# Neighbourhood attention outputs computed by features, with probabilities divided first, in a two-layer hybrid encoder

## What is computed

```python
s = jnp.einsum('brqhd,brkwhd->bhrqkw', qg, k_band) * (d ** -0.5) + bias
s = jnp.where(in_win[:, None, :], s, -jnp.inf)
p = jax.nn.softmax(s.reshape(B, H, rows, GRID_W, kh * GRID_W), axis=-1).reshape(s.shape)
o = jnp.einsum('bhrqkw,brkwhd->brqhd', p.astype(v.dtype), v_band)
...
mixed = jnp.concatenate([ml_out, na_out, gla_out], axis=-1).astype(h.dtype)
return mixed @ w_out
```

## Time and profile before

| | us |
|---|---|
| median of 3 runs (lowest, highest) | 880.56 (879.75, 881.09) |
| profiled execution | 878.24 |
| its span, first to last instruction | 876.3 |
| TensorE busy in the span | 861.8 |
| VectorE busy | 596.0 |
| ScalarE busy | 496.1 |
| mean granted TensorE clock | 0.998 of full speed |

### The profile page before, as it was taken

The page is one execution under the profiler, slowest core; times in us unless marked ns, Lnnn a source line. Parts: engine busy times, 40 slices in busy tenths (PEclk is TensorE's granted clock), DMA queues, the critical chain, the costliest instruction groups (busy, mean ns, idle before and its releaser), DMA issues.

```text
span 876.3 us, 14948 instructions
## 1 busy us (share of the span) xinstructions
PE 861.8 (98%) x6338; PEld 798.1 (91%) x6338; DVE 596.0 (68%) x820; ACT 496.1 (57%) x689; POOL 14.3 (2%) x35
## 2 busy tenths in 40 slices
PE   8999999999999999999999999999999899999997
PEld 8999998889889999999999999988898899999996
DVE  6887678757657666666577885887665666656655
ACT  7954663658647445445567546745755645445444
POOL 5000000000000000000000000000000000000000
PEclk9999999999999999999999999999999999999999
DMA  9735452364255555555448254335435365555541
GB/s 329 201 102 177 156 178 103 112 226 144 97 193 190 195 190 195 192 191 194 145 140 257 72 171 165 127 115 192 135 109 191 127 212 190 193 196 190 192 169 48
DMA packets 114665, 146.78 MB, mean 168 GB/s; under 512 B 10600, under 2 KB 94760, under 8 KB 114600
## 3 DMA queue, kind: packets, MB, share of 16 engines
q1 hardware_dynamic: 114456, 145.57, 49.7%
q10 hardware_dynamic: 144, 0.26, 0.1%
HBM read 144.77 MB, written 1.05 MB: 166 GB/s over the span
## 4 chain that ended last, share of the span: by engine, by line
PE 92%; ACT 3%; DVE 3%; issue 1%; DMA 0%; ACTq 0%; DVEq 0%
PE bank L665 26%; PE bank L666 25%; PE bank L667 25%; PE bank L706 4%; PE bank L743 2%; PE bank L832 2%; DVE wlo L1455 2%; PE bank L1017 2%; ACT whi L1096 1%; ACT yhi L1119 1%; PE bank L872 1%; PE bank L762 1%; PE bank L849 1%; DVE ylo L1710 1%; PE bank L882 1%
## 5 line engine op out<-in xcount | busy, mean ns | idle before, releaser
L1455 DVE TENSOR_TENSOR wlo<-raw,whi 128x2048 fp32r<-128x2048 f32 (+3 forms) x144 | 306.2, 2133 | 106.1 <-ACT whi L1096 105.2
L1096 ACT ACTIVATE whi<-raw 128x2048 fp32r<-128x2048 f32 (+3 forms) x144 | 257.4, 1793 | 53.5 <-PE bank L667 48.4
L665 PE MATMUL bank<-yhi,whi 128*128 128x256 f32 x704 | 195.1, 277 | 0.5 <-DVE ylo L1471 0.5
L666 PE MATMUL bank<-ylo,whi 128*128 128x256 f32 x704 | 194.6, 276 | 0.0
L667 PE MATMUL bank<-yhi,wlo 128*128 128x256 f32 x704 | 194.6, 276 | 0.0
L665 PEld LDWEIGHTS bank<-yhi,whi 128*128 128x128 f32 x704 | 132.2, 188 | 1.6 <-issue 0.7
L666 PEld LDWEIGHTS bank<-ylo,whi 128*128 128x128 f32 x704 | 132.2, 188 | 0.8
L667 PEld LDWEIGHTS bank<-yhi,wlo 128*128 128x128 f32 x704 | 132.2, 188 | 0.0
L665 PE MATMUL bank<-xhi,whi 128*128 128x256 f32 x320 | 91.4, 286 | 2.2 <-DVE wlo L1455 1.2
L665 PE MATMUL bank<-whi,xhi 128*128 128x512 f32 (+2 forms) x256 | 90.1, 352 | 0.0
L667 PE MATMUL bank<-xhi,wlo 128*128 128x256 f32 x320 | 88.9, 278 | 0.0
(11 more groups left out here) (268 smaller groups left out, 1373.1 us busy)
## 6 DMA issues: line engine op xcount, KB each, us to landing
raw<-in_w_up SPq DMA_DIRECT2D x44, 1024.0 KB, 5.0
raw<-in_w_down SPq DMA_DIRECT2D x22, 1024.0 KB, 4.8
raw<-in_w_in SPq DMA_DIRECT2D x10, 1024.0 KB, 7.3
raw<-in_w_xk SPq DMA_DIRECT2D x8, 1024.0 KB, 5.1
raw<-in_w_xv SPq DMA_DIRECT2D x8, 1024.0 KB, 4.9
raw<-in_w_out SPq DMA_DIRECT2D x8, 1024.0 KB, 4.8
raw<-in_w_xq SPq DMA_DIRECT2D x8, 1024.0 KB, 5.7
raw<-in_w_xo SPq DMA_DIRECT2D x8, 1024.0 KB, 4.9
```

The source lines that it names most:

```text
L665: mm(o, s_hi, m_hi, start=first, stop=False, skip_group_check=True)
L666: mm(o, s_hi, m_lo, start=False, stop=False, skip_group_check=True)
L1096: A(weight(whi, gu), raw[:, gu % RING, 0:SIZE[gu]], ACT.Copy).then_inc(hi_done, 1)
L1455: tt(weight(wlo, gu), raw[:, gu % RING, 0:SIZE[gu]], weight(whi, gu), ALU.subtract).then_inc(lo_done, 1)
```

## The change

- Output products. `nao` is no longer one tile a head. Heads (0, 1), (2, 3) and (4) share tiles `nao0`, `nao1`, `nao2`, made at hh = 3, 5 and 6, ahead of that step's transposes. Stationary is `nav` of the head (128 x 64), moving are the transposed probabilities of all 256 queries; the even head's output goes to PSUM partitions 0 to 63, the odd one's to 64 to 127, so features lie on partitions.
- Divisions. VectorE divides the probabilities in SBUF (`shares_of`, two instructions of 128 x 256 a head) before the transposes, which wait for `npn_ready` in place of `np_ready`. The division of the outputs goes.
- Mixer's pair. ScalarE copies each `nao` tile, with the reversal, to `yna_hi` (in the place of `naq`), VectorE subtracts to `yna_lo` (in the place of `nak`, `heads_lo`). `tmb` is no longer transposed for k = 3 and 4, and k = 5 only feeds its upper 64 partitions. `yhi`/`ylo` are made for k = 0, 1, 2, 5, 6, 7; `wo0` begins with k = 3.
- Order. `split_hi` and `split_lo` of the next keys move up by a step (in the second layer `xk3` to hh = 0). The decay exponentials of ScalarE move from hh = 1 to hh = 2, behind the exponentials of heads 2 and 3. VectorE's denominators and head sum move from hh = 0 to hh = 2. In the second layer the GLA decay products and tails move from hh = 2 and 3 to hh = 4, the first pair ahead of the fifth head's division, the rest behind it; in the first layer they stand at hh = 2. `denominators`, `heads_sum`, `decayed` and `tails` hold the same instructions as before.

```diff
+        if h in NA_OUT:
+            p = NA_OUT.index(h)
+            job(f"nao{p}", 4 + p % 2)
         if 1 <= h <= NAH:
             job(f"nat{h - 1}", 2 + (h - 1) % 2)
-        if h >= 2:
-            job(f"nao{h - 2}", 4 + (h - 2) % 2)
...
+NA_OUT = (3, 5, 6)
+NA_PAIRS = ((0, 1), (2, 3), (4,))
+NA_K = range(3, 6)
...
+        def operand(group, k):
+
+            if group == "mx" and k in NA_K:
+                return yna_hi[:, k - 3, :], yna_lo[:, k - 3, :]
+            return tuple(x[:, k, :] for x in PAIR[group])
+
+        def mixed(k):
+
+            r = slice(64, P) if k == 5 else slice(0, P)
+            return (r,) + tuple(x[r] for x in operand("mx", k))
+
+        MIXED_K = (0, 1, 2, 5, 6, 7)
...
+                def input_is(group, kk):
+                    if group == "mx" and kk in NA_K:
+                        is_drained(pe, l, f"nao{kk - 3}")
+                    if group != "mx" or kk in MIXED_K:
+                        lo_is(pe, l, group, kk)
...
+                    if hh in NA_OUT:
+                        p = NA_OUT.index(hh)
+                        is_drained(pe, l, f"nat{NA_PAIRS[p][-1]}")
+                        free(f"nao{p}")
+                        for jt in range(TT):
+                            for g in NA_PAIRS[p]:
+                                r = slice(64 * (g % 2), 64 * (g % 2) + 64)
+                                last = mm(bank(f"nao{p}")[r, 0:T], nav[:, jt, g * DH:(g + 1) * DH], npt[:, g % 2, jt].rearrange("p a b -> p (a b)"),
+                                          start=jt == 0, stop=jt == 1, skip_group_check=True)
+                        last.then_inc(te_done, 1)
                     if 1 <= hh <= NAH:
                         g = hh - 1
-                        pe.wait_ge(np_ready, NAH * l + g + 1)
+                        pe.wait_ge(npn_ready, NAH * l + g + 1)
...
-                    if hh >= 2:
-                        g = hh - 2
-                        is_drained(pe, l, f"nat{g}")
-                        free(f"nao{g}")
-                        for t in range(TT):
-                            for jt in range(TT):
-                                last = mm(bank(f"nao{g}")[:, t * DH:(t + 1) * DH], npt[:, g % 2, t, jt, :],
-                                          nav[:, jt, g * DH:(g + 1) * DH], start=jt == 0, stop=jt == 1)
+                                last = nc.tensor.transpose(bank(f"nat{g}", TT, TT, P)[:, jt, t, :], np_[:, g % 2, t, jt * P:(jt + 1) * P], ident[:])
...
+                        if k not in MIXED_K:
+                            continue
...
-                for n in range(2):
-                    tm_unit(f"wo{n}", (f"wo{n}0", f"wo{n}1"), 512, "mx", n == 0)
+                tm_half("wo0", "a", ("wo00", "wo01"), 512, "mx", True, ks=(3,), first=3, ends=None)
+                tm_half("wo0", "a", ("wo00", "wo01"), 512, "mx", True, ks=(0, 1, 2), first=3, ends=2)
+                tm_half("wo0", "b", ("wo00", "wo01"), 512, "mx", True)
+                tm_unit("wo1", ("wo10", "wo11"), 512, "mx")
...
+                    if hh in NA_OUT:
+                        p = NA_OUT.index(hh)
+                        r = slice(0, 64 * len(NA_PAIRS[p]))
+                        is_filled(act, l, f"nao{p}")
+                        A(forwards(yna_hi[r, p, :]), backwards(bank(f"nao{p}")[r, 0:T]), ACT.Copy).then_inc(na_hi_ready, 1)
...
-                    if hh == 1:
-                        if l == 0:
-                            split_hi("xk1")
-                        else:
-                            split_hi("xk3")
-                        act.wait_ge(bc_ready, l + 1)
-                        A(b1[:], zc, ACT.Exp, scale=1.0 / 16).then_inc(eb_ready, 1)
-                        A(b3[:], zc, ACT.Exp, scale=-1.0 / 16).then_inc(eb_ready, 1)
...
+                    if hh == 2:
+                        act.wait_ge(bc_ready, l + 1)
+                        A(b1[:], zc, ACT.Exp, scale=1.0 / 16).then_inc(eb_ready, 1)
+                        A(b3[:], zc, ACT.Exp, scale=-1.0 / 16).then_inc(eb_ready, 1)
...
+                        split_hi("xk3" if l else "xk1")
                         take("gg1")
...
+                for k in MIXED_K:
                     is_filled(act, l, f"mx_{k % 4}")
-                    if k >= 4:
+                    if k - 4 in MIXED_K:
                         lo_is(act, l, "mx", k - 4)
-                    for r, v in mixed_parts(k):
-                        last = A(forwards(yhi[r, k, :]), v(turned_bank(l, "mx", k)[r, :]), ACT.Copy, scale=pcol[r, R_MG + k:R_MG + k + 1])
-                    last.then_inc(xhi_ready, 1)
+                    r, hi, _ = mixed(k)
+                    A(hi, turned_bank(l, "mx", k)[r, :], ACT.Copy, scale=pcol[r, R_MG + k:R_MG + k + 1]).then_inc(xhi_ready, 3 if k == 5 else 1)
...
+                def shares_of(g):
+                    dve.wait_ge(np_ready, NAH * l + g + 1)
+                    link(V.reciprocal(nsum[:, 2 * g:2 * g + 2], nsum[:, 2 * g:2 * g + 2]))
+                    for t in range(TT):
+                        last = ts(np_[:, g % 2, t, :], np_[:, g % 2, t, :], nsum[:, 2 * g + t:2 * g + t + 1], None, ALU.mult)
+                    last.then_inc(npn_ready, 1)
+
+                def heads_lo(p):
+                    dve.wait_ge(na_hi_ready, 3 * l + p + 1)
+                    r = slice(0, 64 * len(NA_PAIRS[p]))
+                    drain(tt(forwards(yna_lo[r, p, :]), backwards(bank(f"nao{p}")[r, 0:T]), forwards(yna_hi[r, p, :]), ALU.subtract))
...
-                    if hh == 2:
-                        dve.wait_ge(eb_ready, 2 * l + 2)
-                    if hh >= 2:
-                        g = hh - 2
-                        dve.wait_ge(np_ready, NAH * l + g + 1)
-                        link(V.reciprocal(nsum[:, 2 * g:2 * g + 2], nsum[:, 2 * g:2 * g + 2]))
-                        is_filled(dve, l, f"nao{g}")
-                        for t in range(TT):
-                            last = ts(tmb[:, t, ML + g * DH:ML + (g + 1) * DH], bank(f"nao{g}")[:, t * DH:(t + 1) * DH],
-                                      nsum[:, 2 * g + t:2 * g + t + 1], None, ALU.mult)
-                        drain(last)
...
+                        for g in NA_PAIRS[0]:
+                            shares_of(g)
                         split_lo("xk2" if l else "xk0")
                         memory_lo("mem", l, range(KT))
-                        link(tt(hr[:, :, 0:DH], hr[:, :, 0:DH], den[:].rearrange("p (n o) -> p n o", o=1).broadcast_to([P, 24, DH]), ALU.mult))
-                        link(tt(mlh, hraw[:, :, 0, :, 0:DH], hraw[:, :, 1, :, 0:DH], ALU.add))
+                        split_lo("xk3" if l else "xk1")
                     if hh == 1 and l == 0:
-                        split_lo("xk1")
+                        split_lo("xk2")
                     if hh == 2:
-                        if l:
+                        denominators()
+                        for g in NA_PAIRS[1]:
+                            shares_of(g)
+                        heads_sum()
+                        if l == 0:
+                            decayed(0)
+                            decayed(1)
+                            tails()
                             split_lo("xk3")
-                        is_drained(dve, l, "gk")
-                        for d in range(2):
-                            tt(b2[:, 2 * d:2 * d + 2, :], gq[:], b1[:, 2 * d:2 * d + 2, :], ALU.mult)
-                            ins = tt(b3[:, 2 * d:2 * d + 2, :], gk[:], b3[:, 2 * d:2 * d + 2, :], ALU.mult)
-                        link(ins)
-                        if l == 0:
-                            split_lo("xk2")
                     if hh == 3:
-                        for d in range(2):
-                            cv = lambda v: v[:, 2 * d:2 * d + 2, :].rearrange("p a (c n) -> p (a c) n", n=LG)
-                            e = cv(b1)[:, :, (LG - 1) * (1 - d):(LG - 1) * (1 - d) + 1]
-                            last = tt(cv(b4), cv(b3), e.broadcast_to([P, 2 * NCH, LG]), ALU.mult)
-                        last.then_inc(qd_ready, 1)
-                        if l == 0:
-                            split_lo("xk3")
+                        heads_lo(0)
                     if hh == 4 and l == 0:
                         head_squares(mlh, sq, 0, MLH)
                     if hh == 4:
+                        if l:
+                            decayed(0)
+                        shares_of(4)
+                        if l:
+                            decayed(1)
+                            tails()
                         split_lo("xv0a")
-                    if hh == 5 and l:
-                        head_squares(mlh, sq, 0, MLH)
+                    if hh == 5:
+                        if l:
+                            head_squares(mlh, sq, 0, MLH)
+                        heads_lo(1)
...
                 drain(V.tensor_copy(kty[:].rearrange("p a b c -> p (a b) c"), bank("kt1", 4, P)[:, :, 0:32]))
+                heads_lo(2)
...
```

(46 more changed lines are left out.)

29 lines of the change are left out of this document (16 added, 13 removed).

## The result

The changed kernel takes 882.43 us (median; 880.30 to 883.73), the kernel before 879.94 (878.07 to 882.41) beside it: a ratio of 1.0027, interval 1.0016 to 1.0037. It is slower by 0.27%, 2.4 us by the ratio and 2.5 between the medians. The prediction said 878.8, 1.7 under the kernel before, and a range of 877.2 to 881.0; 882.43 lies above it.

The account below looks back on a forecast made before the run. TensorE, busy 98% of the span, was taken to bound the kernel. First layer -0.8 - 0.76, second +0.6 - 0.74, together -1.7: 880.56 - 1.7 = 878.8 us, range 877.2 to 881.0.

Parts of the forecast that it names:

- Part 1: Output products, each layer: three groups of 1.10 replace five of 0.84; TensorE's stream 0.8 us shorter, range 0.4 to 1.3.
- rival (b): Pair groups' two halves don't run side by side: 1.95 for 1.10 us a group, 881.4 us in all; chance 0.09.
- Part 2: Divisions ahead of the transposes: nothing charged; head 4 in the first layer has only 0.7 us of cover.
- Rival (c): Head 4's division late, or ScalarE's new copies hold its exponentials; TensorE also stops in first layer: 879.6 us; chance 0.14.
- Part 3: Key low parts one head ahead: in the second layer a 0.5 us TensorE stop goes, with 0.2 of shorter waits.
- Part 4: VectorE's chain late in second layer: TensorE stops 2.1 to 2.2 us for kt1 before state products, 0.6 lost.
- Rival (d): The 2.2 us stop in the second layer drops the clock to 1.2 GHz behind it: 883 us; chance 0.05.
- Part 5: Mixer's split and projection: four transposes and a stop go, 0.76 us in the first layer, 0.74 in the second.

Follow-up runs that it names:

- e3: The changed kernel with the GLA decay products and tails back at hh = 2 in the second layer: 881.03 us, ratio 1.0023 to the kernel before.
- e7: e2 with VectorE's split of xk3 back from hh = 0 to hh = 2 in the second layer: 877.46 us, ratio 0.9986 to the kernel before.
- e1: The changed kernel with the low part of nao1 right behind the decay tails in the second layer: 879.47 us, ratio 1.0001 to the kernel before.
- e2: e1 with the second layer's head squares behind the state products and ScalarE's root behind its xv0_0 copy: 875.80 us, ratio 0.9951 to the kernel before.
- e5: e2 with a pair's four products issued head by head, not in turn: 875.91 us, ratio 0.9972 to the kernel before.
- e4: The changed kernel with 19 unused identity products in TensorE's stop before kt0, second layer: 879.84 us, ratio 0.9994 to the kernel before.

## Why the prediction was wrong

**What bounds, and the method.** Right. TensorE's stream decides: its stretches account for the whole difference of the two spans.

**Part 1, the output product.** The mechanism was right, the sum in part by luck. Timeline of TensorE in the changed kernel, L0, a pair and the single head with what follows each:

```profile
123.23 1.08 PE L890 MATMUL bank<-arena,nav 128*64 128x256 f32 x8
124.24 0.66 PE L899 MATMUL bank<-ident,arena 128*128 128x128 f32 x4
139.34 1.08 PE L890 MATMUL bank<-arena,nav 128*64 128x256 f32 x4
140.35 0.66 PE L926 MATMUL bank<-ident,arena 128*128 128x128 f32 x4
```

A group takes 1.01 to the next, forecast 1.10. That eight passes of a pair take no longer than four of the single head shows the halves side by side: rival (b) is out. L0 gained 0.75, forecast 0.8, but out of two sizes that were off and cancel: in the chain of the changed kernel the three groups are 0.09 cheaper each than forecast, and the transposes behind each take 0.58 or 0.59 where they take 0.44 behind other products (0.45 for L900 behind the old output product). That is 0.43 to 0.45 a layer; the prediction allowed 0.1. 4.20 - 3.03 - 0.43 is 0.74.

**Part 2, divisions ahead of the transposes.** Right: no transpose of the changed kernel waits for a division in either layer. The cover was as thin as forecast: in L0 the fifth head's division is done at 135.44 and its transposes begin at 135.93, 0.5 later; in L1 it is 564.18 and 564.58. e3 and e7 put more of VectorE's work ahead of divisions (3.6 us of GLA products, a split of some 2.2), and TensorE stopped 1.71 and 1.2. Rival (c) did not come, but its place was real.

**Part 3, key low parts.** No wait at the keys, as forecast. The loop of L1 came out 1.74 shorter where the parts gave 1.5 (0.8 and 0.7). In e7 the old place costs 1.2, at the transposes.

**Part 4, VectorE in L1: here the prediction failed.** The chain itself was added up well. I had the low part of `nao1` done near 570.8 (561.1 + 0.1 + its steps down to the low part, 9.6), and it was done at 571.09, in a profile whose scores start 0.40 later. The step that failed is the next one: "copies kt0 and kt1 0.8". I let VectorE take the two copies behind the low part and let TensorE run on to the state products, stopping only for `kt1`: "a stop of 2.1 to 2.2". I never asked whether TensorE may write `kt0` at all. The bank plan has the answer (`job` gives each tile its bank, `free` waits for the tile before it there): `kt0` follows `nao1` in bank 5, and `kv0` follows `nao2` in bank 4. Before, the last reader of those tiles was the short division of the outputs, long done; after, it is the low part, which the same chain has at its end. So the stop stands ahead of `kt0`, not ahead of the state products, and the 2.7 us of work between the two (568.34 to 571.04 before) no longer fill it. By my own numbers it could have been had: state products reached at 569.5, so the first transposes at 566.8; low part done at 570.8; a stop of 4.0. Measured 4.20. The forecast stop itself was real: with the bank free in time, e1 has it at 2.22, all but 0.33 of it for the copy of `kt1`.

**Rival (d), the clock.** I gave it 0.05, since a stop of 2.2 seemed short against the 3.3 us of idle time at the end of the kernel. With 4.20 that argument turns round. Its mechanism was right and its size near: "four microseconds of work would take eight", measured 3.2 more. That its 883 lies so close to 882.43 is luck, since it leaves out 2.1 us of stop and 0.8 of gain that came on top. And e1, with one stop of 2.22, shows the fall in its profile, so even my own 2.2 was not safe. The 3.3 of the earlier trace rows is when the clock fell, read as if it were the least that brings it down; the rows do not say that.

**Part 5, mixer and projection.** Right in kind, too small: -1.18 and -1.15 for -0.76 and -0.74. Two sizes were off. The stop ahead of the second half stands as 0.32 in the idle column, and I took it at that. Timeline of TensorE in the kernel before, the last product ahead of it:

```profile
172.09 0.39 PE L667 MATMUL bank<-whi,ylo 128*128 128x512 f32 x1
```

From there to 172.79 are 0.70, where 0.23 is usual from product to product, and the next one follows after 0.34: the stop cost some 0.6. The transposes, timeline of TensorE in the changed kernel:

```profile
166.32 1.47 PE L1006 MATMUL bank<-ident,tmb 128*128 128x128 f32 x12
167.54 0.48 PE L684 MATMUL bank<-whi,yna_hi 128*128 128x512 f32 x1
```

Twelve take 1.22 to the projection where sixteen took 1.77: 0.55 less, not 0.44. That makes 1.15 together.

**Sum.** With the wait of `kt0` (+4.2 in place of +2.1), the clock (+3.2) and part 5 (-0.8 more) the forecast's -1.7 becomes: L0 -0.8 - 1.2, L1 -1.7 + 4.2 + 3.2 - 1.2 = +2.5. Measured +2.4.

## What to carry to other kernels

The failed step and the lesson are one. When a change gives a tile a new last reader, or moves that reader, write down for each buffer that it touches who takes it next, and ask of that one whether it is now late: a bank's next user may be a group that has nothing to do with the edit. Price a stop of TensorE twice, once for its length and once for the clock behind it. And before giving up a change that lost, look at what stands between the late step and its predecessor: here two reorderings that add no instruction turned +0.27% into -0.49% (e2); e5, whose stretches take the same time, came to -0.28%, so the gain is some 0.3 to 0.5%.

## What the runs showed of the hardware

The granted clock fell behind a single stop of 4.20 (the changed kernel, 0.9 us after its end), within a stop of 2.22 (e1, 1.1 us after its start, behind 2.0 us of small products at full clock), and behind two of 1.71 and 2.01 with 2.4 us of work between them (e3, 1.5 us after the second: its window 569 to 571 is at 0.78). So the length of a stop alone does not say whether the clock falls, nor when; the runs do not settle what does. It stayed up through 4.4 us of identity products (e4) and a stop of 0.37 (e2). Once down it was so for some 7 us (572 to 579) although TensorE was busy throughout, and that cost 3.2 us.

The clock also falls where no stop is. Windows of the changed kernel early in the program, with TensorE busy all the time:

```profile
28.00:30.00 2.00, 2.00 (x12) 1.64 (x11) 1.97 (x6) 1.99 (x5) 0.00 (x0) 0.85 0.92 270
30.00:32.00 2.00, 2.00 (x12) 2.00 (x11) 1.43 (x2) 2.00 (x2) 0.00 (x0) 0.50 0.87 184
32.00:34.00 2.00, 2.00 (x16) 2.00 (x16) 2.00 (x2) 1.98 (x2) 0.00 (x0) 0.80 0.83 182
```

This is most of the +2.07 of the account: the three windows lack 0.30, 1.00 and 0.40 us of full clock, 1.7 together. The change does not touch that part of the program, and executions of the kernel before scatter alike: of 29, those with a mean clock above 0.997 have a median of 878.76 us, the others 880.19. What brings the clock down there was not tried and stays open, as does whether the share of such executions differs between the two kernels; the comparison of medians holds both. The eleven executions of the changed kernel have mean clocks of 0.991 to 0.995, where 28 of those 29 have 0.996 or more, in keeping with a fall in L1 in each of the eleven.

Two column products of 64 on different halves of one bank overlap whether they are written in turn or one head after the other (1.01 and 1.02 us for eight passes). I had expected the second order to cost. The Trainium skill, "TensorEngine Tiling (Array Packing)", section "Stationary-Streaming Swap + Column Tiling", promises up to twofold for this edit; per pass the trace agrees (eight passes in the time of four), while the three groups a layer took 3.0 us and not the 2.1 of the estimate worked out from it: about 0.2 is paid in each beside its passes, and the transposes behind each take 0.15 more.
